# Norms around an output projection: sums added up on VectorE, the inverse root as an exponential of a logarithm, and half of the projection placed ahead of the second rms norm

## The reference

```python
m = concatenate([rms_norm(o_a, mix_g[:512]), rms_norm(o_b, mix_g[512:])], axis=-1) @ w_out
h = layer_norm(ALPHA * x + m, ln1_g, ln1_b)
f = peer(h, w_q, sub_keys, u_tab, v_tab)      # product-key router, 128 x 128 experts
y = layer_norm(ALPHA * h + f, ln2_g, ln2_b)
# rms_norm: x * rsqrt(mean(x^2) + eps) * g;   layer_norm: (x - mu) * rsqrt(var + eps) * g + b
```

## Time and profile before

| | |
|---|---|
| median of 3 runs | 1116.89 us (1115.89 to 1117.94) |
| profiled execution, its time | 1112.11 us |
| profiled execution, its span | 1110.4 us |
| PE / DVE / ACT / POOL busy | 1065.4 / 865.0 / 551.2 / 260.1 us |

### The profile page before, as it was taken

The page is one execution under the profiler, slowest core; times in us unless marked ns, Lnnn a source line. Parts: engine busy times, 40 slices in busy tenths (PEclk is TensorE's granted clock), DMA queues, the critical chain, the costliest instruction groups (busy, mean ns, idle before and its releaser), DMA issues.

```text
span 1110.4 us, 23617 instructions
## 1 busy us (share of the span) xinstructions
PE 1065.4 (96%) x7264; PEld 953.6 (86%) x7264; DVE 865.0 (78%) x1808; ACT 551.2 (50%) x1054; POOL 260.1 (23%) x281
## 2 busy tenths in 40 slices
PE   6999989979999999999999999989999999999996
PEld 6997646969999999999999999978777787888875
DVE  4325364668988988888459999969888998987877
ACT  5325556344544444434555555545455555555543
POOL 0244302000001000554000000025455554533320
PEclk9999998989999999999999999999999999999998
DMA  7656921423468766999863444459889998977762
GB/s 259 268 192 194 346 92 48 170 77 116 153 209 280 251 232 232 346 413 397 312 218 119 142 142 142 142 186 307 306 288 302 306 300 294 302 243 246 243 215 90
DMA packets 96249, 253.19 MB, mean 228 GB/s; under 512 B 11424, under 2 KB 44224, under 8 KB 95408
## 3 DMA queue, kind: packets, MB, share of 16 engines
q1 hardware_dynamic: 81840, 196.84, 52.1%
q0 software_dynamic: 14368, 55.87, 13.9%
HBM read 232.60 MB, written 22.12 MB: 229 GB/s over the span
## 4 chain that ended last, share of the span: by engine, by line
PE 79%; DVE 7%; DMA 6%; issue 4%; POOL 2%; ACT 2%; DVEq 0%; SPq 0%; ACTq 0%; POOLq 0%
PE ps L557 14%; PE ps L558 14%; PE ps L559 14%; PE ps L990 7%; PE ps L992 7%; PE ps L991 7%; PE ps L971 5%; DMA activations<-u_out 4%; DVE w_lo L1360 3%; PE ps L641 1%; DVE sacc L1804 1%; POOL vrow L518 1%; PE ps L917 1%; POOL a_in L522 1%; DMA a_in<-activations 1%
## 5 line engine op out<-in xcount | busy, mean ns | idle before, releaser
L1360 DVE TENSOR_TENSOR w_lo<-ring,w_hi 128x512 fp32r<-128x512 f32 (+1 forms) x458 | 433.5, 956 | 111.6 <-ACT w_hi L1044 96.5
L1044 ACT CAST w_hi<-ring 128x512 fp32r<-128x512 f32 (+1 forms) x460 | 343.4, 751 | 97.5 <-PE ps L992 51.7
L557 PE MATMUL ps<-h_hi,w_hi 128*128 128x256 f32 (+1 forms) x1152 | 339.3, 295 | 6.0 <-DVE h_lo L1631 4.9
L558 PE MATMUL ps<-h_lo,w_hi 128*128 128x256 f32 (+1 forms) x1152 | 328.7, 285 | 0.0
L559 PE MATMUL ps<-h_hi,w_lo 128*128 128x256 f32 (+1 forms) x1152 | 326.8, 284 | 0.0
L557 PEld LDWEIGHTS ps<-h_hi,w_hi 128*128 128x128 f32 x1152 | 219.6, 191 | 10.7 <-DVE h_lo L1631 5.3
L558 PEld LDWEIGHTS ps<-h_lo,w_hi 128*128 128x128 f32 x1152 | 219.1, 190 | 0.0
L559 PEld LDWEIGHTS ps<-h_hi,w_lo 128*128 128x128 f32 x1152 | 217.3, 189 | 0.0
L990 PE MATMUL ps<-w_hi,y_hi 128*128 128x512 f32 x512 | 201.4, 393 | 11.3 <-DVE y_lo L1792 10.4
L992 PE MATMUL ps<-w_lo,y_hi 128*128 128x512 f32 x512 | 199.8, 390 | 0.0
L991 PE MATMUL ps<-w_hi,y_lo 128*128 128x512 f32 x512 | 199.7, 390 | 0.0
(11 more groups left out here) (337 smaller groups left out, 1216.4 us busy)
## 6 DMA issues: line engine op xcount, KB each, us to landing
ring<-in_uT_dram SPq DMA_DIRECT2D x128, 512.0 KB
ring<-in_v_dram SPq DMA_DIRECT2D x128, 512.0 KB
activations<-u_out SPq DMA_DIRECT2D x128, 128.0 KB
a_in<-activations SPq DMA_DIRECT2D x128, 128.0 KB
ring<-in_w_in_dram SPq DMA_DIRECT2D x22, 512.0 KB
ring<-in_w_q_dram SPq DMA_DIRECT2D x16, 512.0 KB
ks<-in_cache_sb_dram POOLq DMA_DIRECT2D x16, 256.0 KB, 3.2
vs<-in_cache_sb_dram POOLq DMA_DIRECT2D x16, 256.0 KB, 5.5
```

Source lines behind the costliest of these rows:

```text
L557: mm(out, hi, hi_, start=start, stop=False)
L558: mm(out, hi, lo_, start=False, stop=False)
L1044: nc.scalar.copy(w_hi[slot][:, x], ring[:, ring_slot, x]).then_inc(part_hi, 2 if half is None else 1)
L1360: V.tensor_tensor(w_lo[slot][:, x], ring[:, ring_slot, x], w_hi[slot][:, x].bitcast(F32), ALU.subtract).then_inc(part_lo[ring_slot], 2 if ...
```

## The change

- The sums of squares of both rms norms are added up on DVE (`squares_added`: three additions of 128x288, each waiting for the one before); PE then needs one call on ones.
- ACT makes the inverse root straight from the sum, as exp(-0.5 * ln(sum / n + eps)) (`deviation`). DVE's division step and reciprocal, ACT's root and its table load go.
- The first rms norm's chain, `scaled`, `o_hi` and `o_low` of tiles 0 to 3 stand ahead of the sample tokens' copies; the casts of the first two `w_out` tiles stand inside the attention loop of ACT. The other two stay behind `os_`.
- PE runs two weight tiles over features 0 to 3 ahead of `rms_sums(1)`, and the other two behind it.
- Layer norm: DVE adds `xTs` and its squares up tile by tile during the projection (two additions per tile; ACT squares the uncentered tiles). The variance is mean of squares minus square of the mean. Two single calls on ones stand at the end. Four of the eight subtractions stand between the scales.
- Router queries: three weight tiles at once, by feature tile; first the 48 matmuls with `h_hi`, then the 24 with `h_lo`. `scores(0)` and `scores(1)` then stand together, without a projection between them.

The diff, without context and without some removed bodies:

```diff
...
+    c["eps"] = np.full((128, 1), EPS)
...
+        mean = at("mean", [128, T], o + 2 * T)
+        mean2 = at("mean2", [128, T], o + 3 * T)
...
-                for j in range(4):
-                    pe.wait_ge(rm_sq, 4 * m + j + 1)
-                    ins = mm(ps[:, (7, 3)[m], 0:T], k("ones"), sqb[:, 4 * m + j, :], start=j == 0, stop=j == 3)
-                ins.then_inc(rm_mm, 1)
+                pe.wait_ge(rm_add, m + 1)
+                mm(ps[:, (7, 3)[m], 0:T], k("ones"), sqb[:, 4 * m, :], start=True, stop=True).then_inc(rm_mm, 1)
...
+            first_tiles(range(2), range(4))
...
-            pe.wait_ge(ns_o, 1)
-            first_tiles(range(4), range(4))
+            first_tiles(range(2, 4), range(4))
...
+            pe.wait_ge(ln_s, 1)
+            mm(ps[:, 0, 0:T], k("ones"), srow[:, :], start=True, stop=True).then_inc(ln_mm, 1)
+            pe.wait_ge(ln_q, 1)
+            mm(ps[:, 1, 0:T], k("ones"), rrow[:, :], start=True, stop=True).then_inc(ln_v, 1)
...
-            for c in range(2):
-                project((AT_Q + c) % 4, h_parts, c, halves(0, AT_Q + c), x_low=h_l)
+            for kd in range(KD):
+                pe.wait_ge(h_h, kd + 1)
+                for c in range(3):
+                    if kd % 4 == 0:
+                        lows = halves(0, AT_Q + c)
+                        pe.wait_ge(lows[0], lows[1 + kd // 4])
+                    slot, block_ = (AT_Q + c) % 4, slice(kd * 128, (kd + 1) * 128)
+                    mm(ps[:, c, 0:T], w_hi[slot][:, block_], h_hi[:, kd, :], start=kd == 0, stop=False)
+                    mm(ps[:, c, 0:T], w_lo[slot][:, block_], h_hi[:, kd, :], start=False, stop=False)
+            for kd in range(KD):
+                pe.wait_ge(h_l, kd + 1)
+                for c in range(3):
+                    ins = mm(ps[:, c, 0:T], w_hi[(AT_Q + c) % 4][:, kd * 128:(kd + 1) * 128], h_lo[:, kd, :],
+                             start=False, stop=kd == KD - 1)
+                    if kd == KD - 1:
+                        ins.then_inc(w_mm, 2)
...
-                project((AT_Q + c + 2) % 4, h_parts, (c + 2) % 4, halves(0, AT_Q + c + 2))
+                if c >= 1:
+                    project((AT_Q + c + 2) % 4, h_parts, (c + 2) % 4, halves(0, AT_Q + c + 2))
...
+                if u >= 6:
+                    high_of(AT_OUT + u - 6)
...
-            high_of(AT_OUT)
-            act.wait_ge(rm_sd, 1)
-            A(srow[:, :], srow[:, :], ACT.Sqrt).then_inc(rm_sd, 1)
-            high_of(AT_OUT + 1)
+            def deviation(out, sums, n):
+                link(A(out, sums, ACT.Ln, scale=1.0 / n, bias=k("eps")))
+                return A(out, out, ACT.Exp, scale=-0.5)
+
+            act.wait_ge(rm_mm, 1)
+            deviation(srow[:, :], ps[:, 7, 0:T], 512).then_inc(rm_sd, 1)
+            for c in range(4):
+                act.wait_ge(rm_on, c + 1)
+                nc.scalar.copy(o_hi[:, c, :], oT[:, c, :]).then_inc(o_h, 1)
...
+            high_of(AT_OUT + 2)
...
+            act.wait_ge(rm_mm, 2)
+            deviation(rrow[:, :], ps[:, 3, 0:T], 512).then_inc(rm_sd, 1)
...
-            for n in range(AT_OUT, AT_Q):
-                high_of(n + 4, 2 * AT_OUT + 4 + n - AT_OUT + 1 if n < AT_OUT + 4 else 2 * (n + 1))
-
...
+            for c in range(KD):
+                n = AT_OUT + c
+                high_of(n + 4, 2 * AT_OUT + 4 + c + 1 if c < 4 else 2 * (n + 1))
+                act.wait_ge(m_pre, c + 1)
+                A(sqb[:, c, :], xTs[:, c, :], ACT.Square).then_inc(ln_sq, 1)
+            act.wait_ge(ln_mu, 1)
+            A(mean2[:, :], mean[:, :], ACT.Square).then_inc(ln_mu2, 1)
+            act.wait_ge(ln_sd, 1)
+            deviation(rrow[:, :], mean2[:, :], 1).then_inc(ln_sd, 1)
...
-            norm_act(0, xTs, 2, h_hi, h_h)
+            for c in range(KD):
+                act.wait_ge(ln_g, c + 1)
+                A(h_hi[:, c, :], xTs[:, c, :], ACT.Identity, bias=vec[:, 2, c:c + 1]).then_inc(h_h, 1)
...
+            def squares_added(m):
+                t = sqb[:, 4 * m, :]
+                for j in range(1, 4):
+                    dve.wait_ge(rm_sq, 4 * m + j + 1)
+                    ins = V.tensor_tensor(t, t, sqb[:, 4 * m + j, :], ALU.add)
+                    if j < 3:
+                        link(ins)
+                ins.then_inc(rm_add, 1)
+
+            squares_added(0)
...
-            dve.wait_ge(rm_mm, 1)
-            V.tensor_scalar(srow[:, :], ps[:, 7, 0:T], 1.0 / 512, EPS, ALU.mult, ALU.add).then_inc(rm_sd, 1)
-            dve.wait_ge(rm_sd, 2)
-            link(V.reciprocal(srow[:, :], srow[:, :]))
+            dve.wait_ge(rm_sd, 1)
+            for c in range(4):
+                scaled(c)
+                if c >= 1:
+                    o_low(c - 1)
+            o_low(3)
...
-
-            for c in range(4):
-                scaled(c)
-                if c >= 2:
-                    o_low(c - 2)
-            o_low(2)
-            o_low(3)
-            dve.wait_ge(rm_mm, 2)
-            V.tensor_scalar(rrow[:, :], ps[:, 3, 0:T], 1.0 / 512, EPS, ALU.mult, ALU.add).then_inc(rm_sd, 1)
-            dve.wait_ge(rm_sd, 4)
-            link(V.reciprocal(rrow[:, :], rrow[:, :]))
+            squares_added(1)
+            dve.wait_ge(rm_sd, 2)
...
-                if c >= 6:
-                    o_low(c - 2)
-            o_low(6)
+                if c >= 5:
+                    o_low(c - 1)
...
+            def squares_summed(c):
+                dve.wait_ge(ln_sq, c + 1)
+                if c == 1:
+                    link(V.tensor_tensor(rrow[:, :], sqb[:, 0, :], sqb[:, 1, :], ALU.add))
+                elif c < KD - 1:
+                    link(V.tensor_tensor(rrow[:, :], rrow[:, :], sqb[:, c, :], ALU.add))
+                else:
+                    V.tensor_tensor(rrow[:, :], rrow[:, :], sqb[:, c, :], ALU.add).then_inc(ln_q, 1)
+
...
+                dve.wait_ge(m_pre, c + 1)
+                if c == 1:
+                    link(V.tensor_tensor(srow[:, :], xTs[:, 0, :], xTs[:, 1, :], ALU.add))
+                elif 1 < c < KD - 1:
+                    link(V.tensor_tensor(srow[:, :], srow[:, :], xTs[:, c, :], ALU.add))
+                elif c == KD - 1:
+                    V.tensor_tensor(srow[:, :], srow[:, :], xTs[:, c, :], ALU.add).then_inc(ln_s, 1)
+                if c >= 2:
+                    squares_summed(c - 1)
...
+            squares_summed(KD - 1)
+
+            def center(c):
+                V.tensor_tensor(xTs[:, c, :], xTs[:, c, :], mean[:, :], ALU.subtract).then_inc(ln_c, 1)
+
+            def stretch(c):
+                dve.wait_ge(ln_c, c + 1)
+                V.scalar_tensor_tensor(xTs[:, c, :], xTs[:, c, :], vec[:, 1, c:c + 1], rrow[:, :],
+                                       ALU.mult, ALU.mult).then_inc(ln_g, 1)
...
-            norm(0, xTs, 1, lambda c: h_low(c - 2) if c >= 2 else None)
-            h_low(KD - 2)
-            h_low(KD - 1)
+            dve.wait_ge(ln_mm, 1)
+            V.tensor_scalar(mean[:, :], ps[:, 0, 0:T], 1.0 / D, None, ALU.mult).then_inc(ln_mu, 1)
+            dve.wait_ge(ln_mu, 1)
+            dve.wait_ge(ln_sq, KD)
+            center(0)
+            center(1)
+            dve.wait_ge(ln_mu2, 1)
+            dve.wait_ge(ln_v, 1)
+            link(V.scalar_tensor_tensor(srow[:, :], ps[:, 1, 0:T], 1.0 / D, mean2[:, :], ALU.mult, ALU.max))
+            V.tensor_tensor(mean2[:, :], srow[:, :], mean2[:, :], ALU.subtract).then_inc(ln_sd, 1)
+            center(2)
+            center(3)
+            dve.wait_ge(ln_sd, 2)
+            for c in range(KD):
+                stretch(c)
+                if c < 4:
+                    center(c + 4)
+                else:
+                    h_low(c - 4)
+            for c in range(4, KD):
+                h_low(c)
```

More of the change, by code:

```diff
@@ L335, in trunk @@
         np_free = sem("np_free")
+        rm_add, ln_s, ln_q, ln_mu, ln_mu2 = map(sem, ("rm_add", "ln_s", "ln_q", "ln_mu", "ln_mu2"))
         np_qk, np_s, np_e, np_p, np_t, np_pt, np_pv, np_o = map(sem, (
@@ L1201, in _ @@
                 A(sqb[:, c, :], oT[:, c, :], ACT.Square).then_inc(rm_sq, 1)
-            for c in range(4):
-                act.wait_ge(rm_on, c + 1)
-                nc.scalar.copy(o_hi[:, c, :], oT[:, c, :]).then_inc(o_h, 1)
-            high_of(AT_OUT + 2)
-            act.wait_ge(rm_sd, 3)
-            A(rrow[:, :], rrow[:, :], ACT.Sqrt).then_inc(rm_sd, 1)
             high_of(AT_OUT + 3)
+            act.wait_ge(rm_mm, 2)
+            deviation(rrow[:, :], ps[:, 3, 0:T], 512).then_inc(rm_sd, 1)
             for c in range(4, KD):
```

33 lines of the change are left out of this document (removed).

## The result

The changed kernel takes 1114.28 us, median of 20 runs (1107.22 to 1119.04); the kernel before took 1118.02 in 20 runs on the same chip (1114.21 to 1127.98). The ratio of the means is 0.994, interval 0.992 to 0.997: faster by 6.4 us by the means (1120.4 to 1114.0), by 3.7 us by the medians. The forecast was 1108.1 us, own range up to 1111.5. In this and later ratios, runs more than 1.5% above the fastest run of the same kernel are left out; medians and means keep them.

The account below looks back on a forecast made before the run. TensorE, busy 96% of the span, was taken to set the pace. Gains of 1.5 (rms norms) and 8.0 us (layer norm) less 0.7 (router) make 8.8, so 1116.89 - 8.8 = 1108.1 us; range 1103.5 to 1111.5.

Parts of the forecast that it names:

- The level: Base of the sum: median of the runs before the change, 1116.89 us, 4.8 us above the profiled execution of 1112.11.
- a clock that is down for more than 7 us at a time: Sign named in advance that the forecast would be wrong: TensorE at reduced clock for over 7 us in one stretch.
- The first rms norm: Ahead of the output projection: shorter chain lets PE begin 24 projection matmuls at 186.0 instead of 190.75 us, `os_` not delayed.
- The second rms norm: Within the projection: DVE's additions wait twice for POOL, ending at 192.4; 97th matmul 1.5 us earlier, bounds -0.3 to +3.1.
- Rival C: More half clock, in the 24 matmuls at the second rms call and 6.8 us in the router stretch: 1111.3 us; chance 0.2.
- The layer norm: From last projection matmul to first router matmul: 6.6 us instead of 14.64, gain 8.0 us, bounds 7.3 and 8.5.
- The router's first tiles: From first router matmul to fourth tile: 14.95 us instead of 14.2 with 5.15 us at half clock, loss 0.7 us.
- The rest of the projection: Later projection tiles: DVE's turn about 2.6 us against PE's 3.2 us per tile, so it costs nothing.
- B: At the second rms norm, DVE not held by POOL or only once: 1106.5 us, 1104 if the clock stays up; chance 0.27.
- A: The forecast itself: two waits for POOL, half clock behind the layer norm; 1108 us, range 1106 to 1110; chance 0.45.
- D: Gain eaten behind the stage, as top-16 starts later and transfers meet in another phase; 1117 us if all lost; chance 0.05.
- E: Slower: DVE's longer turn bounds the projection, needing 4.8 us per turn; 1119 us; chance 0.03.

Follow-up runs that it names:

- a_warm_att: The changed kernel with eighteen idle TensorE calls on ones added in the attention stage; median 1110.0 us, ratio to the kernel before 0.988 to 0.995.

## Why the prediction was wrong

**The level.** The step that failed is the sum's base, "the median of the runs is 4.8 us above that execution, and 1116.89 - 8.8". That median was of three runs of a kernel that spreads over 20 us (1111.5 to 1131.7); over 142 runs the mean is 1120.5, and all three lay with the fast group. The level accounts for 3.6 of the 6.2 us by which the median missed. The rest, 2.5 us, is gain that the runs don't show: 6.3 us where the sum says 8.8. Under a steady clock it is 7.9, and 8.8 lies within its uncertainty. The split depends on the measure: by the medians of the first comparison alone, the level is 1.1 us and the missing gain 5.1. The prediction's own sign of being wrong, a clock that is down for more than 7 us at a time, came true (17 us), but ahead of the stage, where its sum had no term.

**The first rms norm** went as put: first `w_out` matmul 0.34 us behind the last transposes' start, `os_` not delayed. Ahead of it, PE's wait for `ptcs` (0.87 us) stands where it had the calls on ones.

**The second rms norm** had the right mechanism. Forecast: third addition's end 6.9 us behind the last transposes' start (192.4 - 185.49), projection 1.5 us shorter. Measured: 6.77 us (204.84 - 198.07) and 1.64 us shorter. The Trainium skill ("SBUF — State Buffer", section "SBUF: two separate sides") has VectorE with two SBUF operands wait for GpSimd's whole instruction; the trace agrees: 4.61 against 1.43 us and 3.50 against 0.95 in the new cases, each ending 0.3 us behind POOL. The trace of before has a second such case, which the prediction passed over: the first scale (186.66, 0.62 us in place of 0.51) started beside this instruction of POOL and ended 0.31 behind it.

```profile
184.62 2.35 POOL L502 TENSOR_TENSOR w_lo<-ring,w_hi 128x1024 fp32r<-128x1024 f32 x1 [0.31 <-ACT w_hi L1044]
```

What the term missed is that it holds for one draw of the clock, so that its 1.64 us were partly luck. Where PE is fast through the 24 matmuls it waits 3.2 us, falls to half clock behind that, and the 1.5 us become -1.1 (a_warm_att). Rival C's "new wait of PE ahead of the second rms call makes 24 matmuls slow" is this mechanism.

**The layer norm**: 6.77 us for a forecast of 6.6, gain 7.87 for 8.0. But its cause was mis-assigned. With the router's order on PE undone it is 9.75 us: 3 us of the 8.0 hang on PE's taking the `h_hi` products first while DVE makes the low parts late, and are lost without it. The prediction counted steps up to the first `h_hi` only.

**The router's first tiles**: 14.12 us for 14.95; no loss. Half clock from 235.28 to 239.28 cost 2.0 us for 2.6; from the first `scores` (247.21) to the fourth tile took 2.19 us for 2.75. And the term "loss 0.7" named only the stretch behind the first product: from the projection's end on, the order gains 2.6 to 3.5 us by the marks.

**The rest of the projection** cost nothing, as put: no wait for `w_lo` in 170 to 300 us; DVE's turn was 2.66 us, under PE's 3.2.

**Rivals.** B is out (the additions are held, and the clock does fall). C's long half clock behind the norm did not come (4.0 us, not 6.8); its time, 1111.3, is closer to the measured one than A's, but not for its reason. D: nothing is eaten behind the stage (from the fourth tile to the end 863.70 us against 863.98). E: out, by the turn above.

What stays open: which of its short waits and narrow matmuls sends the clock down in the attention stage in a given execution, whether the change makes that a little more frequent, and why the experts' last product takes 367 us in some executions and 372 in others.
